# Compression pages loaded ahead, the first product in two parts in front of the barrier, a shorter gates' tile, and input rows reloaded later

## What is computed

```
parts = split(rmsnorm(x, ln_pre_mix) @ w_in)   # rq rk rv rg nq ck cv sk sv wk wv gt
gates = sigmoid(gt)                            # 8 heads x 3 branches = 24 columns
def compress(rows, pos_emb, w1, w2):           # rows: blocks of 64 tokens
    blk = rows.reshape(B, nb, 64, G, d) + pos_emb[:, None, :]
    h = gelu(einsum('bnlgd,ldf->bngf', blk, w1))
    return einsum('bngf,fd->bngd', h, w2)
kc = compress(concat([gather_pages(cache_cmp_k, page_table), ck], 1), cmp_pos_k, cmp_w1_k, cmp_w2_k)
vc = compress(concat([gather_pages(cache_cmp_v, page_table), cv], 1), ...)
o  = gates0 * attend(q, kc, vc) + gates1 * selected + gates2 * window
x  = finish(x, retention_out(...), o, w_o, ...)    # w_o, residual with x, norm, MLP, norm
```

## Time and profile before

| | |
|---|---|
| median of 3 runs | 1750.71 us (1748.14 to 1752.81) |
| profiled execution, its own time | 1747.43 us |
| its span | 1745.8 us |
| TensorE matmul, weight load | 94%, 83% of the span |
| VectorE, ScalarE, GpSimd | 61%, 40%, 12% |
| mean granted TensorE clock | 0.979 |

### The profile page before, as it was taken

One profiled execution on the slowest core, in us unless ns is written; L12 is line 12 of the kernel. 1 busy time (PEld: TensorE's weight loads), 2 busy tenths in 40 slices (PEclk: granted clock), 3 DMA queues, 4 the chain that ended last, 5 costly groups with the idle time before them and its releaser, 6 DMA issues. The chain is left out here.

```text
span 1745.8 us, 31453 instructions
## 1 busy us (share of the span) xinstructions
PE 1634.9 (94%) x12256; PEld 1445.0 (83%) x12256; DVE 1062.7 (61%) x1841; ACT 692.7 (40%) x1270; POOL 213.5 (12%) x305
## 2 busy tenths in 40 slices
PE   4999999998799778999998999999999999999997
PEld 4989989998564465655556999999999999999997
DVE  5566362121114626777886777877767788797576
ACT  5222323211001117666664676533333443433343
POOL 1000000001543220000000010033222000000011
PEclk9999999999899889999999999999999999999999
DMA  8111111142886450000005556533433753443465
GB/s 305 49 38 50 37 38 44 37 103 74 223 221 188 126 134 0 1 1 1 1 1 150 165 166 196 159 116 134 148 138 137 276 183 126 178 147 122 125 173 162
DMA packets 206838, 204.05 MB, mean 117 GB/s; under 512 B 15325, under 2 KB 175666, under 8 KB 203106
## 3 DMA queue, kind: packets, MB, share of 16 engines
q1 hardware_dynamic: 170930, 154.33, 28.4%
q0 software_dynamic: 12720, 37.21, 6.9%
q10 hardware_dynamic: 23040, 10.50, 2.3%
HBM read 163.27 MB, written 42.89 MB: 118 GB/s over the span
## 5 line engine op out<-in xcount | busy, mean ns | idle before, releaser
L2469 PE MATMUL psum<-right_hi,left_hi 128*128 128x258 f32 x1088 | 308.2, 283 | 3.3 <-issue 2.7
L2469 PE MATMUL psum<-right_hi,left_lo 128*128 128x258 f32 x1088 | 308.0, 283 | 0.0
L2469 PE MATMUL psum<-right_lo,left_hi 128*128 128x258 f32 x1088 | 307.7, 283 | 0.0
L235 PE MATMUL psum<-act_hi,whi 128*128 128x344 f32 x648 | 214.0, 330 | 4.0 <-DVE act_lo L408 4.0
L2469 PEld LDWEIGHTS psum<-right_hi,left_hi 128*128 128x128 f32 x1088 | 206.3, 190 | 3.7 <-issue 2.9
L235 PE MATMUL psum<-act_hi,wlo 128*128 128x344 f32 x648 | 207.6, 320 | 0.0
L235 PE MATMUL psum<-act_lo,whi 128*128 128x344 f32 x648 | 207.4, 320 | 0.0
L2469 PEld LDWEIGHTS psum<-right_lo,left_hi 128*128 128x128 f32 x1088 | 206.4, 190 | 0.0
L2469 PEld LDWEIGHTS psum<-right_hi,left_lo 128*128 128x128 f32 x1088 | 206.4, 190 | 0.0
L235 PEld LDWEIGHTS psum<-act_hi,whi 128*128 128x128 f32 x648 | 122.3, 189 | 11.4 <-DVE act_lo L408 4.4
L235 PEld LDWEIGHTS psum<-act_lo,whi 128*128 128x128 f32 x648 | 122.3, 189 | 0.4
(11 more groups left out here) (441 smaller groups left out, 3605.2 us busy)
## 6 DMA issues: line engine op xcount, KB each, us to landing
hidden_forms<-pair_out SPq DMA_DIRECT2D x84, 258.0 KB, 2.4
right_raw<-hidden_forms SPq DMA_DIRECT2D x21, 1032.0 KB, 4.8
wraw<-in_w_in SPq DMA_DIRECT2D x27, 512.0 KB, 3.7
pair_raw<-in_w_up SPq DMA_DIRECT2D x13, 1024.0 KB, 5.5
down_weights<-in_w_down SPq DMA_DIRECT2D x12, 1024.0 KB, 8.0
last_raw<-in_w_down SPq DMA_DIRECT2D x24, 512.0 KB, 4.0
tail_raw<-in_w_o SPq DMA_DIRECT2D x23, 512.0 KB, 4.2
tail_raw<-in_w_up SPq DMA_DIRECT2D x18, 512.0 KB, 4.5
```

The source lines that it names most:

```text
L235: last = pe.matmul(out, w[:, kt, :], x[:, kt, :], start=(kt == 0 and n == 0), stop=(kt == KT - 1 and n == 2))
L2469: last = pe.matmul(ps[:, first_bank(at) + e, 0:HT // 2], wt[:, kt, :], xt[:, kt, cols], start=(opens and kt == 0 and i == 0), stop=(kt == ...
```

## The change

In the projection SP now loads 28 of the 64 pages of round 0 behind w1, into room where the rope and decay tables had been. Of the other 36 each of the three queues loads 12, and after them the pages of round 1, in the old shares. TensorE computes the first product still in this stage, in two parts: the 56 columns of the 28 pages, then the other 89. GpSimd copies the prompt's rows ahead of its pages; its clearing of two tiles moves behind the barrier. The gates' tile puts the low part of its 24 columns into 24 unused columns of the high part, so two products a block give both; nine products with a 128 x 24 matrix of ones and zeros add and transpose, and the sigmoid comes last on ScalarE. In the cache stage SP loads w1 of V first, and the gates' way through DRAM stands behind the pages of round 2. In the tail GpSimd waits for tile 2 before it asks for x.

```diff
-    SHARES = {"sp": (0, 24), "act": (24, 24), "pool": (48, 16)}
+    AHEAD = 28
+    SHARES = {"sp": (28, 12), "act": (40, 12), "pool": (52, 12)}
+    NEXT_SHARES = {"sp": (0, 24), "act": (24, 24), "pool": (48, 16)}
...
+    def products(self, pe, ps):
+        ahead = self.ahead[:].rearrange("p q (g d) -> p (q g) d", g=G)
+        cut = G * self.AHEAD
+        pe.wait_ge(self.w1_loaded, 32)
+        pe.wait_ge(self.ahead_loaded, 16 * self.AHEAD)
+        for part in range(2):
+            if part:
+                pe.wait_ge(self.pos_loaded, 32)
+                pe.wait_ge(self.prompt_in, 1)
+                for who, (_, count) in self.SHARES.items():
+                    pe.wait_ge(self.pages_loaded[who], 16 * count)
+            cols = slice(cut, 145) if part else slice(0, cut)
+            for d in range(HD):
+                for h in range(2):
+                    rows, to = slice(h * HD, (h + 1) * HD), (h + d) % 2
+                    src = (self.slots if part else ahead)[rows, cols, d]
+                    last = pe.matmul(ps[to * HD:(to + 1) * HD, 2 * (d % 2), cols], self.w1[rows, d, :], src, start=(d < 2), stop=(d >= HD - 2))
+        last.then_inc(self.hidden_made, 1)
...
@@ projection, SP
             early.load_w1(sp)
+            early.load_ahead(sp)
             sp.wait_ge(w.tile_done, 3 * len(COLUMNS) + 6)
             early.load_pos(sp)
             early.load(sp, "sp")
+            early.load_next(sp, "sp")
@@ projection, TensorE
+            def gates_chunk(t):
...
+                    for n, x in enumerate((w.x_hi, w.x_lo)):
+                        last = pe.matmul(ps[:, t, 0:TN], m.whi[LAST % 2][:, kt, :], x[:, kt, chunk(t)], start=(kt == 0 and n == 0),
+                                         stop=(kt == KT - 1 and n == 1))
...
+            early.products(pe, ps)
@@ projection, ScalarE
-                    evacuate(TAIL0 + c, t, tmpF, ACT.Sigmoid if c == 6 else ACT.Copy)
+                    evacuate(TAIL0 + c, t, tmpF)
             early.load(act, "act")
+            early.load_next(act, "act")
+            act.wait_ge(feat_copied, 14)
+            act.activation(m.gate_tok[:, 0:NB, :], m.gate_tok[:, 0:NB, :], ACT.Sigmoid).then_inc(gates_ready, 1)
+            act.activation(m.gate_tok[0:DEC, NB, :], m.gate_tok[0:DEC, NB, :], ACT.Sigmoid).then_inc(gates_ready, 1)
@@ projection, GpSimd
-            early.load(pool, "pool")
             pool.wait_ge(normed, 12)
             early.prompt_keys(pool)
+            early.load(pool, "pool")
+            early.load_next(pool, "pool")
@@ cache, SP
+            sp.dma_start(w1[1][0:HD], io["cmp_w1_v"][0]).then_inc(w1_loaded[1], 16)
...
-            sp.dma_start(scratch, m.gate_tok[0:DEC, NB, :]).then_inc(gates_out, 16)
-            load_round(sp, "sp", 1)
-            sp.dma_start(w1[1][0:HD], io["cmp_w1_v"][0]).then_inc(w1_loaded[1], 16)
-            sp.wait_ge(gates_out, 16)
-            sp.dma_start(gates[:, 0:3], scratch.rearrange("b (h c) -> (b h) c", c=3)).then_inc(gates_in, 16)
             sp.wait_ge(hidden_made, 1)
...
             load_round(sp, "sp", 2)
+            sp.dma_start(scratch, m.gate_tok[0:DEC, NB, :]).then_inc(gates_out, 16)
+            sp.wait_ge(gates_out, 16)
+            sp.dma_start(gates[:, 0:3], scratch.rearrange("b (h c) -> (b h) c", c=3)).then_inc(gates_in, 16)
             sp.wait_ge(hidden_made, 2)
@@ cache, TensorE
-            first_product(0)
             first_product(1)
@@ tail, GpSimd
+            pool.wait_ge(raw_loaded[2], 16)
             load_x(0)
```

More of the change, by code:

```diff
@@ L475, in __init__ @@
         self.slots = self.slab[:].rearrange("p q (g d) -> p (q g) d", g=G)
+        self.ahead = m.place("slab0_pages_ahead", [P, self.AHEAD, P], F32, m.tables)
+        self.next_slab = m.place("slab1_pages", [P, 64, P], F32, m.A + 73 * 512)
+        assert m.tables + self.AHEAD * 512 <= m.const_at("kdec")
         self.w1 = m.place("w1_k", [P, HD, HD], F32, m.M + 4 * TOK * 4)
@@ L501, in prompt_keys, with load_ahead, load_next @@
         pool.tensor_copy(self.slots[:, 128:144, :], m.ck_tok[:, 0:NB, :].rearrange("p b (g d) -> p (b g) d", g=G)).then_inc(self.prompt_in, 1)
-        pool.memset(m.kcpT[:], 0.0).then_inc(self.zeroed, 1)
-        pool.memset(m.vcp[:], 0.0).then_inc(self.zeroed, 1)
+    def load_ahead(self, sp):
+        sp.wait_ge(self.table_loaded, 16)
+        load_pages(self.nc, sp, self.table, 0, self.AHEAD, self.io["cache_cmp_k"][0],
+                   lambda k: self.ahead[:, k:k + 1, :], self.ahead_loaded)
+    def load_next(self, eng, who):
+        first, count = self.NEXT_SHARES[who]
+        load_pages(self.nc, eng, self.table, 64 + first, count, self.io["cache_cmp_k"][0],
+                   lambda k: self.next_slab[:, first + k:first + k + 1, :], self.next_loaded[who])
+    def products(self, pe, ps):
[16 more added lines that the diff above has]
+        last.then_inc(self.hidden_made, 1)
     def load(self, eng, who):
@@ L561, in stage_project @@
         tmpF = m.feat
+        GATES = NH * 3
+        fold = m.place("gates_fold", [P, GATES], F32, m.stage + 9248)
+        assert m.stage + 9344 <= int(nc.sbuf_usable_end)
+        folds, gates_ready = s("gate_folds"), s("gates_ready")
+        LAST = 26
         PAIRS = NB // 2
@@ L734, in _ @@
                     variance(j, 5, NB + 1)
+            def gates_chunk(t):
+                if t == 0:
+                    pe.wait_ge(w.hi_ready, LAST + 1)
+                    pe.wait_ge(w.lo_ready, LAST + 3)
+                pe.wait_ge(w.bank_free, LAST * 3 + (t + 1))
+                for kt in range(KT):
+                    for n, x in enumerate((w.x_hi, w.x_lo)):
+                        last = pe.matmul(ps[:, t, 0:TN], m.whi[LAST % 2][:, kt, :], x[:, kt, chunk(t)], start=(kt == 0 and n == 0),
+                                         stop=(kt == KT - 1 and n == 1))
+                last.then_inc(w.tile_done, 1)
             for c in range(7):
                 for t in range(3):
-                    w.multiply_chunk(pe, TAIL0 + c, t)
+                    if c == 6:
+                        gates_chunk(t)
+                    else:
+                        w.multiply_chunk(pe, TAIL0 + c, t)
                     if c == 0 and t == 0:
@@ L745, in _ @@
                     pe.wait_ge(normed, 12)
+                if c == 6:
+                    pe.wait_ge(folds, 1)
+                    for i in range(NB):
+                        pe.matmul(ps[:, 3, i * GATES:(i + 1) * GATES], tmpF[:, i * P:(i + 1) * P], fold[:], start=True, stop=True)
+                    pe.matmul(ps[0:DEC, 4, 0:GATES], tmpF[:, SEQ:TOK], fold[:], start=True, stop=True).then_inc(feat_turned, 1)
+                    continue
                 for i in range(NB):
@@ L1075, in take @@
             return dc[:, lo:hi]
[L1077 removed]
+        ROUND_SHARES = early.NEXT_SHARES
         def load_round(eng, who, n):
```

32 lines of the change are left out of this document (19 added, 13 removed).

## The result

The changed kernel takes **1735.97 us** (median of 7 executions, 1731.66 to 1741.40), against 1751.36 for the kernel before on the same chip: a ratio of 0.9916, 95% interval 0.9901 to 0.9930, or 14.7 us less. A second set, with the same kernel as one of the experiments, gave 0.9910 (0.9894 to 0.9925). The profiled execution took 1735.97 us itself, with a span of 1734.3 (before: 1745.8).

A forecast was written before the change was run, and what follows sets the result against it. Bound by TensorE's series of work and gaps, chiefly page issuing before a barrier; 12.8 us at the V product plus 1.7 in the tail gave 14.5 off 1747.4, so 1732.9, plus 3.3 to the median: 1736 us, range 1731 to 1743.

The forecast's parts named there:

- Gates' tile: Tile before the first K product: 48 matmuls for 72, 3.8 us less, T at 425.3; fold products priced like transposes.
- Part ahead: First 56 columns of the first K product: 31 ns a record, 8.0 us, hidden beside the issue of the remaining pages.
- Rest: Other 89 columns: start at T + 14.4 when GpSimd's twelfth page lands, 50 ns a record, 12.7 us, end T + 27.2.
- The width rival: First product's parts: a matmul costs the same at any width, making the kernel 2.3 us slower, 1753; chance 0.05.
- The barrier: Before the second K product: TensorE arrives last, the crossing takes 3.55 us as before, product starts at T + 30.8, 456.1.
- the reading that the gap was issuing and not the pages' time: 18.3 us gap before the first K product: time spent issuing page transfers in front of a barrier.
- V product: First V product: starts 24.0 us behind TensorE's start after the barrier, bounds 22.3 and 25.1; at 480.1, 12.8 us earlier.
- the transfer rival: Around the barrier: transfers bound it, GpSimd's last page 3.5 us later, V pages and gate rows 3 more; 1742.7, chance 0.15.
- Gate rows: Before the second V product: SP's store and read-back, 5 us of landing, stay hidden with 1.6 us of cover.
- Tail: w_o products in the tail: asking for x later lands tile 2 sooner, gaining 1.7 us of idle time; bounds 0 and 1.7.
- the rigid shift: After the V product: the same work follows in the same order, so all of it moves by the same amount.
- The clock's rule: Product after idle gaps: its pace doesn't follow TensorE's clock, so nothing is charged; the opposing rival had 1738, chance 0.06.

The follow-up runs named there:

- run 4: Changed kernel with the gates' tile as before, three products a block and nine transposes; ratio 0.9929 to the kernel before.
- run 7: Changed kernel with GpSimd copying the prompt rows behind its 12 pages instead of ahead of them; ratio 0.9906 to the kernel before.
- run 3: Changed kernel with no page loaded ahead, shares 24, 24, 16 and one 145-column product in front of the barrier; 1749.57 us, ratio 0.9991.
- run 8: Changed kernel with round 2, the first 64 V pages, shared SP 20, ACT 28, GpSimd 16 instead of 24, 24, 16; ratio 0.9925.
- run 1: Changed kernel without GpSimd's wait for w_o tile 2 in the tail; ratio 0.9923 to the kernel before.
- run 2: Kernel before with only GpSimd's wait in the tail added; ratio 1.0006 to the kernel before.
- run 5: Changed kernel with both parts of the first product moved behind the barrier, pages still loaded ahead; 1754.15 us, ratio 1.0028.
- run 9: Changed kernel with 24 identity-matrix products filling TensorE's wait for the V pages; 1737.54 us, ratio 0.9931.
- run 10: Changed kernel with SP asking for w1 of V in front of the barrier, behind its last page; 1733.6 us, ratio 0.9892.
- run 11: Changed kernel with w1 of V asked for before the barrier and round 2 shared SP 20, ACT 28, GpSimd 16; 1734.7 us, ratio 0.9902.
- run 12: Changed kernel with w1 of V and the four w2 pieces asked for before the barrier, shares as changed; 1734.5 us, ratio 0.9900.

## Why the prediction was right

1736 us forecast, 1735.97 measured. The mechanism is right, and that the two numbers meet is luck in two places: a crossing 1.7 us shorter than forecast makes up for V pages 1.2 us late, and a profiled execution 3.1 us above the forecast one happens to be the median. By its steps, times counted from T:

- *Gates' tile.* T moved from 429.1 to 425.4, as forecast; run 4 gives 3.9 us for the tile. Mis-sized: eight of the fold products, two records each, take 1.97 us where I left them at the transposes' price, of which eight took 1.09 in the kernel before:

```profile
429.66 1.09 PE L747 MATMUL psum<-const,feature_rows 128*128 128x128 f32 x8 [0.55 <-ACT feature_rows L754]
```

- *Part ahead.* 8.35 us for 8.0, 32.6 ns a record; hidden, as forecast.
- *Rest.* 51 ns a record for 50. The second part starts at T + 14.1 for T + 14.4, but by other numbers: GpSimd's twelfth page is issued at T + 9.2, not 10.4, since the copy costs nothing (run 7), and TensorE starts 4.9 us later, not 4.0, as it takes 4.8 us to land. Its end, 452.57, is at T + 27.1 for T + 27.2. The width rival is dead: 56, 89, 128 and 145 columns cost 33, 51, 73 and 82 ns.
- *The barrier.* TensorE came last, as forecast (ACT 451.6, SP 449.8). The crossing was mis-sized: 1.83 us for 3.55. In the kernel before, SP's last page, issued at 445.3, landed only at 448.5, 0.7 us ahead of the first product. So of the 3.55 us most would have been a wait for pages in any case, and the reading that the gap was issuing and not the pages' time leaves this out; run 3 shows the same 18.6 us as a wait for pages. The sum also has no term for the landing of round 1's last page: it landed at 453.9, and the engines left the barrier at 454.2, so it cost nothing by 0.3 us.
- *V product.* 25.2 us behind the K product for 24.0, outside my upper bound of 25.1 by a hair. The bounds were made of issuing, and run 8 shows that issuing isn't what counts here; the transfer rival had the right mechanism in this one place, and its 3 us for it was 1.2.
- *Gate rows.* The store was 4.9 us from issue to the next step, for 5 forecast, and the second V product didn't wait.
- *Tail.* 1.9 us shorter in the profile, for 1.7; the times of runs 1 and 2 leave between nothing and that.

So 13.3 + 1.9 = 15.2 us against 14.5, in line with the 14.7 and 15.8 measured. The same sum from the profiles of all runs follows their ratios (ratio less one, times 1751 us) to within 3.5 us, no closer. T itself lies anywhere from 424.3 to 426.4 in the executions with the short tile, which is noise that the first column carries:

```
run                        V product  tail     sum    measured (+-3; run 1 +-3.6, run 4 +-4.8)
no wait in the tail (1)      -11.7    +1.7   -10.0    -13.5
tail's wait alone (2)         +1.1    -2.3    -1.2     +1.1
nothing ahead (3)             +2.8    -1.7    +1.1     -1.6
gates' tile as before (4)     -8.3    -1.9   -10.2    -12.4
behind the barrier (5)        +5.8    -1.8    +4.0     +4.9
changed kernel               -13.3    -1.9   -15.2    -14.7
changed kernel again (6)     -14.6    -1.9   -16.5    -15.8
copy behind (7)              -11.4    -1.9   -13.3    -16.5
round 2 shared anew (8)      -14.2    -2.0   -16.2    -13.1
wait filled (9)              -13.2    -2.1   -15.3    -12.1
w1 of V ahead (10)           -15.9    -1.9   -17.8    -18.9
and shares of run 8 (11)     -16.2    -2.4   -18.6    -17.2
and w2 ahead (12)            -16.3    -1.7   -18.0    -17.5
```

*The step that failed is the rigid shift.* In the profile itself only 11.5 of the 15.2 us arrive, because from the V product to the attention's first product the same work took 152.8 us (479.57 to 632.41) where it took 149.1 before (492.88 to 642.01). The other stretches cancel: from there to the first w_o product it is 1.2 us longer, behind the row sums 1.1 us shorter. My sum met the median all the same. I had the profiled execution at 1732.9 and the median 3.3 us above it; it came out at 1735.97, and the median is the same. That the lost 3.7 us aren't the change's is likely and not shown: the profiled execution before had a mean granted clock of 0.979, near the upper end of that kernel's 43 executions in the experiments' sets (0.971 to 0.980, mean 0.975), while eleven of the changed kernel have 0.971 to 0.982, mean 0.977. Most of the difference shows in the granted clock of the 12 us that begin 40 us behind the V product's start. In turn the kernel before, run 5, runs 10 and 9, and the changed kernel:

```profile
532.88:544.88 12.00, 9.24 (x40) 0.86 0.43 124
```

```profile
538.67:550.67 12.00, 9.04 (x40) 0.86 0.43 118
```

```profile
517.00:529.00 12.00, 9.21 (x40) 0.72 0.38 109
```

```profile
519.65:531.65 12.00, 9.21 (x39) 0.72 0.38 111
```

```profile
519.57:531.57 12.00, 9.24 (x34) 0.62 0.38 109
```

At 0.86 the way to the attention takes 149.1 and 149.5 us, at 0.72 (runs 2, 4, 8, 9, 10 and 11) 150.2 to 150.5, but 152.0 in run 7, and at 0.62 to 0.65 (the changed kernel twice, runs 1, 3 and 12) 152.3 to 153.6. Run 2 has the program of the kernel before up to there, so 1.0 us of this comes with no change at all. In all of them TensorE stands idle for 2.6 to 2.8 us in this stretch, waiting for the GELU, and runs for a part of it at the lower level, 1.2 GHz, and for the rest at the upper, 2.4 GHz; how long is what differs. The shorter and the longer way both occur with the pages ahead and without, with the V wait at 0.5 us (run 9) and at 6.3, at 1.5 both in run 10 (0.72) and in run 12 (0.63). The filler of run 9 therefore explains nothing, since run 8 had 150.4 us without it. What decides how soon the clock returns is open.

*The clock's rule.* The first part ran right behind busy time in the changed kernel and behind 27 idle us in run 5. Its stretches in run 5, and the second part's in the changed kernel (length, busy, records, clock, DMA share, GB/s):

```profile
455.20:457.20 2.00, 2.00 (x65) 0.50 0.64 139
458.00:462.00 4.00, 4.00 (x138) 0.99 0.80 155
```

```profile
440.00:442.00 2.00, 2.00 (x48) 0.61 1.03 286
440.00:452.00 12.00, 12.00 (x248) 0.86 1.06 277
```

65 records in 2 us are 31 ns each at the lower level of 1.2 GHz, 138 in 4 us are 29 ns at the upper. The clock moves this line by 6%. The 89-column part isn't slower at 0.61 (48 records in 2 us, 42 ns each) than over the whole (48 ns). The Trainium skill, "TensorE: Matmul & The Clock Gate", section "Back-to-back issue gap", has the spacing of isolated matmuls about twice as long with the clock halved. That is not what this line shows at 56 or 89 columns either.

## What to carry to other kernels

A gap in front of a barrier is not closed by having the data earlier, nor by moving the work forward alone: in runs 3 and 5 one without the other gained nothing, and together they gave 13 us, because the work then runs beside the issuing that the barrier waits for. When the gap is closed, what is asked for behind the barrier becomes the next bound, so look at what the transfer engines do just before it and start the largest load where they fall quiet. Started earlier, it slows what is still in flight: w1 of V, asked for at 449.8 with the engines busy until 452, gave 4.8 us and took 2.2 back. And a shift of work along one engine carries to the end only as far as the waits on the way find the same clock; judge it by medians, not by the end of one profile.

## What the runs showed of the hardware that was not expected

- The barrier's crossing is no constant. From the last visible work of the last engine to the next work it took 1.4 us (run 3), 1.8 and 2.4 us (run 1) with TensorE last, 3.55 us before, and 5.9 us in run 5, where ACT was done at 449.23, the last page landed at 453.1, and TensorE started at 455.15. It does not wait for transfers: in run 10 the engines went on at 454.5, and a page of round 1 landed at 456.6. What filled it isn't seen.
- A copy of 1.04 us on GpSimd at the head of its page loads cost nothing (run 7).
- Products with 24 moving columns (two records each, eight of them in 1.97 us) cost more than transposes of 128 columns (one record each, eight in 1.09 us).
- The price of a page's issue on ACT isn't fixed: 36 pages took 21.2 us in run 5, 23.7 in the changed kernel, 25.7 in run 4 and 27.0 in run 7, where one page alone took 1.96 us.
- A load of 1 MB just ahead of 64 pages lengthens the landing of each: from 457 to 473 us SP's pages land 7.6 us after their issue in the changed kernel (median), and 4.8 us in run 10, where the load went out 4.4 us sooner.
